# A two-layer streaming encoder: one pair of gate/up tiles moved from the third to the second stage of each feed-forward sublayer

## The reference

```
h   = rms_norm(x, g_pre)
mlp = (silu(h @ w_gate) * (h @ w_up)) @ w_down        # hidden width 2816 = 22 tiles of 128
x   = x + 0.5 * rms_norm(mlp, g_post)                 # the mixers: x + rms_norm(mix(h), g_post)
```

## Time and profile before

| what | us |
|---|---|
| median of 3 runs | 1931.15 |
| lowest, highest | 1929.95, 1933.97 |
| profiled execution, its own time | 1932.5 |
| profiled execution, span from first to last instruction | 1930.4 |
| PE busy in the span | 1912.4 |
| DVE busy | 1299.6 |
| ACT busy | 1060.2 |
| POOL busy | 196.3 |

### The profile page before, as it was taken

The page is one execution under the profiler, slowest core; times in us unless marked ns, Lnnn a source line. Parts: engine busy times, 40 slices in busy tenths (PEclk is TensorE's granted clock), DMA queues, the critical chain, the costliest instruction groups (busy, mean ns, idle before and its releaser), DMA issues.

```text
span 1930.4 us, 38306 instructions
## 1 busy us (share of the span) xinstructions
PE 1912.4 (99%) x15888; PEld 1861.9 (96%) x15888; DVE 1299.6 (67%) x1716; ACT 1060.2 (55%) x2077; POOL 196.3 (10%) x221
## 2 busy tenths in 40 slices
PE   9999999999999999999999999999999999999997
PEld 9999999999669999999999999999997999999997
DVE  7876784574673887578539775883567487758834
ACT  7563665531684656366545653665438556536652
POOL 0000000200352100000020000001236200000011
PEclk9999999999999999999999999999999999999999
DMA  4323323232311222333322223233341222232231
GB/s 161 104 73 107 110 90 97 99 105 77 123 45 45 62 93 83 96 108 109 92 86 77 99 77 121 88 105 96 107 123 41 73 64 99 78 121 89 103 98 65
DMA packets 63627, 177.90 MB, mean 92 GB/s; under 512 B 7569, under 2 KB 16097, under 8 KB 63329
## 3 DMA queue, kind: packets, MB, share of 16 engines
q1 hardware_dynamic: 61328, 167.66, 26.4%
q0 software_dynamic: 2128, 7.80, 1.2%
HBM read 168.26 MB, written 5.36 MB: 90 GB/s over the span
## 4 chain that ended last, share of the span: by engine, by line
PE 94%; DVE 4%; issue 1%; ACT 1%; DMA 0%; POOL 0%; DVEq 0%; ACTq 0%; SPq 0%
PE psum L796 29%; PE psum L794 29%; PE psum L795 29%; PE psum L1129 1%; PE psum L1115 1%; PE psum L1248 1%; DVE y L1952 1%; PE psum L1037 1%; PE psum L1231 1%; DVE rstd L1941 1%; PE psum L1092 1%; PE psum L1203 1%; DVE xlo L2030 0%; DVE w_lo L648 0%; PE psum L1081 0%
## 5 line engine op out<-in xcount | busy, mean ns | idle before, releaser
L794 PE MATMUL psum<-xhi,w_hi 128*128 128x272 f32 x1632 | 473.9, 290 | 0.2
L796 PE MATMUL psum<-xhi,w_lo 128*128 128x272 f32 x1632 | 470.4, 288 | 0.0
L795 PE MATMUL psum<-xlo,w_hi 128*128 128x272 f32 x1632 | 469.6, 288 | 0.0
L796 PE MATMUL psum<-h_hi,w_lo 128*128 128x272 f32 x1216 | 351.0, 289 | 0.0
L795 PE MATMUL psum<-h_lo,w_hi 128*128 128x272 f32 x1216 | 350.0, 288 | 0.0
L794 PE MATMUL psum<-h_hi,w_hi 128*128 128x272 f32 x1216 | 349.5, 287 | 0.0
L794 PEld LDWEIGHTS psum<-xhi,w_hi 128*128 128x128 f32 x1632 | 307.4, 188 | 3.5 <-issue 2.0
L795 PEld LDWEIGHTS psum<-xlo,w_hi 128*128 128x128 f32 x1632 | 307.2, 188 | 0.5
L796 PEld LDWEIGHTS psum<-xhi,w_lo 128*128 128x128 f32 x1632 | 306.7, 188 | 0.0
L648 DVE TENSOR_TENSOR w_lo<-w_raw,w_hi 128x1024 fp32r<-128x1024 f32 (+1 forms) x214 | 184.3, 886 | 163.5 <-ACT w_hi L645 163.0
L645 ACT ACTIVATE w_hi<-w_raw 128x1024 fp32r<-128x1024 f32 (+1 forms) x214 | 160.9, 770 | 216.0 <-PE psum L796 214.0
(11 more groups left out here) (304 smaller groups left out, 3709.9 us busy)
## 6 DMA issues: line engine op xcount, KB each, us to landing
w_raw<-in_w_gate_up SPq DMA_DIRECT2D x172, 512.0 KB, 4.3
w_raw<-in_w_down SPq DMA_DIRECT2D x96, 256.0 KB, 2.8
w_raw<-in_w_down SPq DMA_DIRECT2D x32, 512.0 KB, 3.6
w_raw<-in_even_in SPq DMA_DIRECT2D x16, 512.0 KB, 4.1
w_raw<-in_odd_in SPq DMA_DIRECT2D x10, 512.0 KB, 4.0
w_raw<-in_w_down SPq DMA_DIRECT2D x32, 128.0 KB, 2.6
w_raw<-in_even_out SPq DMA_DIRECT2D x8, 512.0 KB, 4.2
w_raw<-in_odd_out SPq DMA_DIRECT2D x8, 512.0 KB, 4.4
```

Source lines behind the costliest of these rows:

```text
L794: nc.tensor.matmul(out, s_hi, m_hi, start=first, stop=False, skip_group_check=skip)
L795: nc.tensor.matmul(out, s_hi, m_lo, start=False, stop=False, skip_group_check=skip)
L796: return nc.tensor.matmul(out, s_lo, m_hi, start=False, stop=last, skip_group_check=skip)
```

## The change

Two tables of constants change. The second stage takes 8 sevens (4 pairs, 8 tiles) in place of 6, the third 10 (5 pairs, 10 tiles) in place of 12. All loops, load sizes and waits are made from these tables. The second units of the second stage's down pass have 4 tiles in place of 2, those of the third 2 in place of 4. The fourth pair of the second stage stands at the places 10 and 11 of the hidden buffers.

```diff
 PLAIN = 4
-KDOWN = (6, 12)
+KDOWN = (8, 10)
 UNIT = (4, 8)
-HIDDEN = ((0, 1, 2, 3, 8, 9), tuple(range(12)))
+HIDDEN = ((0, 1, 2, 3, 8, 9, 10, 11), tuple(range(10)))
 HELD = 4
 PAIRS = [(f, f + 1) for f in range(PLAIN, KF, 2)]
 SEVEN = 2 * len(PAIRS)
```

## The result

The changed kernel takes 1937.46 us in the median of 16 runs (1934.41 to 1945.67), the kernel before 1931.8 us in as many (1929.95 to 1939.48). The ratio is 1.0028, 95% interval 1.0019 to 1.0038: **slower by 5.4 us, 0.28%**, where 4.65 us, 0.24%, was forecast, inside the range.

A forecast was written before the change was run, and what follows sets the result against it. PE is 99% busy, but at the boundaries behind feed-forward sublayers DVE's chain sets the time and PE has no slack. Median 1931.15 us, +6.75 lost cover, -2.1 gain: 1935.8 us, range 1933.5 to 1939.0.

The forecast's parts named there:

- The boundary has no slack and every lost matmul costs its time: Behind the first three feed-forward sublayers, 18 matmuls leave PE's cover of DVE's chain: 3 x 2.25 = 6.75 us lost.
- First rival: At the boundaries, DVE's chain has slack and absorbs the 2.25 us; only the 2.1 us gain stays, 1929.0 us; chance 0.10.
- What releases PE: At the boundaries, PE meets its waits 2.25 us early: first half 1's sum, then xlo, both hanging on DVE's chain.
- The gain ahead of the third stage: Longer second down pass covers PE's stalls before the third stage's first product: 3 x 0.25 + 1.36 = 2.1 us gained.
- The stall of 0.25 us: PE's stall before the third stage's first product, behind DVE's weight sums, in three sublayers; forecast to vanish wholly.
- The sum: Whole kernel: +6.75 us lost less 2.1 us gained, +4.65 us, giving 1935.8 us, +0.24%.
- third rival: Third down pass's start: ACT is late, its two slacks of 0.2 us being too small; 1937.0 us, up to 1938; chance 0.06.
- The kernel's end at no cost: Behind the fourth feed-forward sublayer, PE waits only for the last output's square: cost 0, upper bound 1.0 us.
- second rival: In the boundaries' new waits the clock falls, 1.7 us each: one gives 1937.5 us, three 1940.9; chance 0.12.
- a stall of 1.36 us without a fall: Second sublayer, ahead of the third stage: a late load's stall brought no clock fall, read as evidence against the second rival.

The follow-up runs named there:

- b_late18: Kernel before with only the sum of half 0's squares 18 matmuls later in PE's order; 1941.88 us, ratio 1.0048.
- a_early12: Changed kernel with the sum of half 0's squares 12 matmuls earlier in PE's order; 1933.18 us, ratio 1.0006 to the kernel before.
- b_early18: Kernel before with the sum of half 0's squares 18 matmuls earlier in PE's order; 1931.99 us, ratio 0.9997.
- b_late36: Kernel before with the sum of half 0's squares 36 matmuls later in PE's order; 1948.62 us, ratio 1.0080.
- a_h1late: Changed kernel with PE's sum of half 1 behind input tile 5 in place of 3; 1937.92 us, ratio 1.0028 to the kernel before.
- b_nowhole: Kernel before (tables 6 and 12) with the early half 0 sum of a_nowhole; 1932.79 us, ratio 1.0000.
- b_sums: Kernel before with the weight sums of the third stage's first product behind the add of output 12, not 13; 1932.87 us, ratio 0.9994.
- a_nowhole: Changed kernel, half 0's sum one output earlier, PE adding the last tile's square in fp32; 1931.42 us, ratio 0.9989 to the kernel before.
- a_nowhole2: a_nowhole run again, beside b_nowhole and the changed kernel on one chip; 1932.57 us, ratio 0.9998 to the kernel before.
- a_third: The changed kernel itself, run a third time; 1937.23 us, ratio 1.0028 to the kernel before.

## Why the prediction was right, point by point

- *The boundary has no slack and every lost matmul costs its time* (+6.75 us): right, 6.8 us in the trace. The stretch is unchanged with 18 matmuls fewer. Taken alone it is 6.7 us (b_late18), given back by 12 it is 4.5 (a_early12), and the other way it brings 1.0 (b_early18). First rival (the cover is kept): refuted. Each trace compared with that of before, matmul by matmul:

| kernel | matmuls behind half 0's sum, against before | later at the three boundaries, us |
|---|---|---|
| b_late36 | 36 fewer (4.5 us) | 4.47, 4.47, 4.40 |
| changed kernel | 18 fewer (2.25 us) | 2.24, 2.30, 2.23 |
| b_late18 | 18 fewer (2.25 us) | 2.21, 3.87 (with a fall of the clock), 2.18 |
| a_early12 | 6 fewer (0.75 us) | 0.80, 0.77, 0.70 |
| b_early18 | 18 more | -0.33, -0.32, -0.38 |

- *What releases PE*: the prediction named POOL's total of half 1 and then xlo, both hanging on DVE's chain. The waits stand where it said, and a_h1late shows that it is the chain that counts and not the total.
- *The gain ahead of the third stage* (2.1 us): right in kind, too small by 0.7 us. The stall of 0.25 us has a second part that the prediction did not count: behind the late product the next matmul starts 0.23 us later in place of 0.125, so it is 0.35 us, three times, and 1.36 + 0.1 us once: 2.5 us. By the two traces the gain is 2.8 us. The 0.08 us more in each sublayer come in small steps in the third stage's products and in its down pass, which the prediction put at nothing; their cause was not tried. The largest single part, in the second sublayer, is as large as the load is late: between the starts there stood 1.49 us in before, 1.19 in b_early18 and 1.24 in b_nowhole.
- *The sum* (+4.65 us): with the gain at the measured 2.8 for 2.1 it is +3.9 us, and that is what the two spans at equal clock give. Executions at a mean clock of 0.998 or more give 1934.77 us (13 of the changed kernel) against 1930.93 us (37 of before), +3.8, and the means of all 34 and 96 executions 1937.25 - 1933.15 = +4.1. So the forecast was 0.7 us too high, and the first comparison's +5.4 us is 1.5 us above the change itself; three comparisons gave +5.4, +2.9 and +5.4. That the first of them came so near to 4.65 is in part luck with the clock.
- *ACT late at the start of the third down pass* (third rival): not seen. No two matmuls of the changed kernel start more than 0.133 us apart between 318 and 345 us, the first sublayer's pass. The put for output 4 ended at 333.65, 1.86 us after the first result, for 1.9 forecast.
- *The kernel's end at no cost*: right; the start of L1011 comes 0.52 us behind the matmul before it, as before.
- *The clock falls in the new waits* (second rival, 0.12): half true, and priced well. It falls in some executions: at 2 of 9 boundaries in the three traces of the changed kernel, and at 1 of 3 in a_h1late and b_late18 each, for 1.3 to 1.7 us. In the changed kernel and b_late18 it followed 3 of the 6 waits of 2.1 us at L1003 and none of the 6 of 1.4 us; in a_h1late one of three waits of 1.7 us. The prediction had read a stall of 1.36 us without a fall as a sign against it; that held for the waits of 1.4 us and not for the longer ones. It falls in none of the 18 boundaries of the six traces in which these waits are missing (before, b_early18, b_sums, b_nowhole, a_nowhole and a_nowhole2). As an addition to the mean it is small: the mean granted clock is 0.99653 in the changed kernel (34 executions) and 0.99671 before (80), 0.3 us by the slope below.

## What to carry to other kernels

When PE is busy for 99% of the span, look for the stretch in which another engine is busy for as long as PE's matmuls last, and count the matmuls that stand between the instruction that starts that engine and the one that waits for it. Work moved out of that stretch costs its full time even though the total of work is the same, while moving the starting instruction forward gives it back. The line at which PE then waits names only the first wait met; move that line, and see whether the time changes, before blaming it. Look up where in time each wait of a list stands: here the longest at xlo was in most traces one at the kernel's start. And where two kernels issue the same matmuls in number, compare their traces matmul by matmul: it settles tenths of a microsecond that a median of twelve executions does not.

## What the runs showed of the hardware beyond what was expected

The spread from one execution to the next (1934.4 to 1945.7 us for the changed kernel) goes mostly with TensorE's clock. Over its first 16 runs, time and mean granted clock have a correlation of -0.98 and a slope of 1700 us for a clock of 1, so about 1.5 us for 3.41 us at 0.50. A smaller part is the kernel's start: the 400th matmul starts at 54.5 us in the earliest of the thirteen traces (a_nowhole2 and a_h1late) and at 55.5 us in the latest (b_nowhole). In the attention, where PE waits often, the traces have from nothing (the changed kernel, a_early12, b_sums, a_h1late) over 3.41 (five traces, before among them) and 6.83 (a_third, b_nowhole) up to 20.48 us at 0.50 (b_late18, b_late36) for the same instructions. A change of 0.2% is therefore seen better among executions of the same mean clock than in the medians of all.
